# A two-layer encoder kernel: one more pair of feed-forward tiles in seven products, and earlier query weights

## The reference, cut to what matters

```python
def swiglu(h, w_gu, w_down):
    u = h @ w_gu
    return (jax.nn.silu(u[..., :D_FF]) * u[..., D_FF:]) @ w_down

def swa_sink_attention(hn, w_q, sinks, w_o, k, v):
    ...
    s = jnp.einsum('bcqkgd,bcwkd->bckgqw', q, kw).astype(jnp.float32) * (HEAD_DIM ** -0.5)
    ...
    m = jnp.maximum(jnp.max(s, axis=-1, keepdims=True), sink)
    p = jnp.exp(s - m)
    p = p / (jnp.sum(p, axis=-1, keepdims=True) + jnp.exp(sink - m))
    o = jnp.einsum('bckgqw,bcwkd->bcqkgd', p.astype(vw.dtype), vw)
    return o.reshape(B, S, N_Q_HEADS * HEAD_DIM) @ w_o
```

## Time and profile before

| | us |
|---|---|
| median of 3 runs | 1071.61 |
| lowest and highest run | 1071.55, 1072.2 |
| the profiled execution's own time | 1071.88 |
| its span, first to last instruction | 1070.1 |
| TensorE busy | 1059.6 |
| VectorE busy | 858.9 |
| ScalarE busy | 618.9 |
| GpSimd busy | 52.3 |

### The profile page before, as it was taken

The page is one execution under the profiler, slowest core; times in us unless marked ns, Lnnn a source line. Parts: engine busy times, 40 slices in busy tenths (PEclk is TensorE's granted clock), DMA queues, the critical chain, the costliest instruction groups (busy, mean ns, idle before and its releaser), DMA issues.

```text
span 1070.1 us, 17761 instructions
## 1 busy us (share of the span) xinstructions
PE 1059.6 (99%) x6817; PEld 953.7 (89%) x6817; DVE 858.9 (80%) x1310; ACT 618.9 (58%) x1127; POOL 52.3 (5%) x86
## 2 busy tenths in 40 slices
PE   8999999999999999999999999999999999999997
PEld 7887887889999999998888988889999999998886
DVE  5878987688888888889877589568888888889874
ACT  6376574555466666656556587555455555556553
POOL 1000000000112222100010100000000000000000
PEclk9999999999999999999999999999999999999999
DMA  6332233242346556462234201152234334352211
GB/s 210 99 109 70 79 110 119 79 118 73 119 135 188 155 171 194 132 228 89 79 99 153 65 2 40 45 152 64 90 105 119 96 103 119 92 201 102 79 40 79
DMA packets 137142, 117.74 MB, mean 110 GB/s; under 512 B 8305, under 2 KB 123105, under 8 KB 137058
## 3 DMA queue, kind: packets, MB, share of 16 engines
q1 hardware_dynamic: 133600, 106.12, 32.1%
q0 software_dynamic: 3456, 10.49, 2.9%
q10 hardware_dynamic: 2, 0.00, 0.0%
HBM read 109.25 MB, written 7.34 MB: 109 GB/s over the span
## 4 chain that ended last, share of the span: by engine, by line
PE 97%; DVE 1%; ACT 1%; issue 0%; DMA 0%; DVEq 0%; ACTq 0%
PE ps L2389 12%; PE ps L2387 12%; PE ps L2385 12%; PE ps L2047 8%; PE ps L2048 8%; PE ps L2049 8%; PE ps L2067 7%; PE ps L2073 7%; PE ps L2069 7%; PE ps L2103 4%; PE ps L2101 4%; PE ps L2102 4%; PE ps L2316 1%; PE ps L2080 1%; PE ps L2491 1%; PE ps L2519 1%
## 5 line engine op out<-in xcount | busy, mean ns | idle before, releaser
L2385 PE MATMUL ps<-t_hi,w_hi 128*128 128x256 f32 x608 | 172.1, 283 | 0.0
L2387 PE MATMUL ps<-t_lo,w_hi 128*128 128x256 f32 x608 | 172.1, 283 | 0.0
L2389 PE MATMUL ps<-t_hi,w_lo 128*128 128x256 f32 x608 | 172.1, 283 | 0.0
L2047 PE MATMUL ps<-x_hi,w_hi 128*128 128x512 f32 (+1 forms) x384 | 137.1, 357 | 0.3 <-DVE w_lo L1382 0.2
L2048 PE MATMUL ps<-x_lo,w_hi 128*128 128x512 f32 (+1 forms) x384 | 135.1, 352 | 0.0
L2049 PE MATMUL ps<-x_hi,w_lo 128*128 128x512 f32 (+1 forms) x384 | 135.0, 352 | 0.0
L1382 DVE TENSOR_TENSOR w_lo<-raw,w_hi 128x1024 fp32r<-128x1024 f32 x73 | 89.0, 1223 | 54.2 <-ACT w_hi L836 53.9
L2389 PE MATMUL ps<-x_hi,w_lo 128*128 128x256 f32 x456 | 129.0, 283 | 0.0
L2387 PE MATMUL ps<-x_lo,w_hi 128*128 128x256 f32 x456 | 129.0, 283 | 0.0
L2385 PE MATMUL ps<-x_hi,w_hi 128*128 128x256 f32 x456 | 129.0, 283 | 0.0
L2385 PEld LDWEIGHTS ps<-t_hi,w_hi 128*128 128x128 f32 x608 | 116.7, 192 | 0.0
(11 more groups left out here) (288 smaller groups left out, 2587.5 us busy)
## 6 DMA issues: line engine op xcount, KB each, us to landing
raw<-in_ffn_w_gu SPq DMA_DIRECT2D x88, 512.0 KB, 4.8
raw<-in_ffn_w_down SPq DMA_DIRECT2D x28, 512.0 KB, 4.2
raw<-in_a_w_in SPq DMA_DIRECT2D x24, 512.0 KB, 3.9
raw<-in_a_w_out SPq DMA_DIRECT2D x12, 512.0 KB, 3.9
scaled_kv_q<-part POOLq DMA_DIRECT2D x20, 256.0 KB, 3.8
part<-in_b_w_q POOLq DMA_DIRECT2D x32, 128.0 KB, 2.8
xr<-in_ffn_w_down SPq DMA_DIRECT2D x8, 512.0 KB, 7.7
raw<-in_b_w_o SPq DMA_DIRECT2D x16, 256.0 KB, 4.0
```

What stands on the lines that cost most here:

```text
L2047: nc.tensor.matmul(out_ps, hi_w, hi_x, start=first, stop=False)
L2385: nc.tensor.matmul(ps[:, b, 0:HS], w_hi[:, slot, cols], hi, start=start, stop=False, skip_group_check=True)
L2387: nc.tensor.matmul(ps[:, b, 0:HS], w_hi[:, slot, cols], lo, start=False, stop=False, skip_group_check=True)
L2389: ins = nc.tensor.matmul(ps[:, b, 0:HS], w_lo[:, slot, cols], hi, start=False, stop=j == DC // 2 - 1, skip_group_check=True)
```

## The change

1. PLAIN is 2 instead of 3: in each layer the third plain pair becomes the first in seven products, so there are 20 of these. The banks follow: `seven_banks(c)` gives 0, 1, 2, then 3, 4, 5, then 6, 7, 2 for the first three pairs, and the pairs behind alternate as before. The sums of x_f's first half and two weight sums are now made in the boundary (`whole_x`, `weight_sum_3`, `weight_sum_2`), ahead of the last x_low.
2. The low halves of tiles T+2 and T+3 of each layer are no longer subtracted on VectorE. ScalarE writes the rounded negative of the tile into `w_lo`, and a DMA from GpSimd's queue adds `raw` to it. TensorE and SyncE wait for that DMA (w_lo_landed). ScalarE's split of T+3 goes ahead of x_high(b, 2).
3. The query tiles T_Q+2 and T_Q+3 are split around the keys; T_Q+4's cast goes ahead of the table load of the exponential; queries 1 are split on VectorE altogether (`q_both(1, 2)`), row_max(1) goes ahead of the first division, and T_Q+5's cast behind the exponentials.
4. The table of Silu is loaded by a small activation at the start of the feed-forward, and three semaphores of constants are made one.

```diff
-PLAIN = 3
+PLAIN = 2
...
+def low_by_dma(t):
+
+    return any(t - T_GU[f] in (2, 3) for f in range(2))
...
+def seven_banks(c):
+
+    if c == 2:
+        return 6, 7, 2
+    first = 3 * ((c + (c > 2)) % 2)
+    return first, first + 1, first + 2
...
+            def add_raw(t):
+
+                pool.wait_ge(w_neg_ready, dma_lows(t))
+                nc.gpsimd.dma_start(w_lo[:, t % 4, :], raw[:, t % 4, :], accum_op=ALU.add)\
+                    .then_inc(w_lo_landed[t % 4], 16)
+
+            add_raw(T_GU[0] + 2)
+            add_raw(T_GU[0] + 3)
             pool.wait_ge(hid_ready, 2)
...
                     nc.scalar.copy(halves(t)[0], raw_of(t)).then_inc(w_hi_ready, 1)
+                if low_by_dma(t):
+                    nc.scalar.mul(halves(t)[1], raw_of(t), -1.0).then_inc(w_neg_ready, 1)
...
                 post(b, 3)
+                if b != 1:
+                    split_hi(n + 4)
                 x_high(b, 2)
                 pre(b, 3)
-                split_hi(n + 4)
+                if b == 1:
+                    split_hi(n + 4)
                 x_high(b, 3)
...
+            split_hi(T_Q + 2)
             act.wait_ge(tiles_done, upto(T_KV))
             act.wait_ge(kpad_ready, 1)
             nc.scalar.mul(k_hi[:, CHUNK:], bank(0), HD ** -0.5).then_inc(khi_ready, 1)
-            split_hi(T_Q + 2)
+            split_hi(T_Q + 3)
...
             q_high(0)
-            split_hi(T_Q + 3)
+            split_hi(T_Q + 4)
             nc.scalar.activation(std[:, 35:36], eps[:, 0:1], ACT.Exp)
...
             ins.then_inc(vdiag_ready, 1)
-            split_hi(T_Q + 4)
-            q_high(1)
...
                 split_lo(n + 4)
+                if b != 1:
+                    whole_x(b // 2, 0)
+                    weight_sum_3(b // 2, 0)
+                    weight_sum_2(b // 2, 0)
                 x_low(b, 3)
...
+            split_lo(T_Q + 2)
             dve.wait_ge(khi_ready, 1)
...
+            split_lo(T_Q + 3)
+
             def q_both(m, parts):
...
             q_low(0)
-            split_lo(T_Q + 2)
...
                 if half == 0:
-                    q_low(1)
+                    q_both(1, 2)
             biased(1, 0)
             biased(1, 1)
+            row_max(1)
...
             def tile_ready(t):
-                pe.wait_ge(w_lo_ready, upto(t))
+                if low_by_dma(t):
+                    pe.wait_ge(w_hi_ready, upto(t))
+                    pe.wait_ge(w_lo_landed[t % 4], 16 * dma_lows_in_place(t))
+                else:
+                    pe.wait_ge(w_lo_ready, lows_upto(t))
```

More of the change, by code:

```diff
@@ L162, in fixed, with lows_upto, dma_lows, dma_lows_in_place @@
     return len(FIXES) * f + FIXES.index(name) + 1
+def low_by_dma(t):
+    return any(t - T_GU[f] in (2, 3) for f in range(2))
+def lows_upto(t):
+    return sum(pair_of_seven(i) is None and chunk_place(i) is None and not low_by_dma(i) for i in range(t + 1))
+def dma_lows(t):
+    return sum(low_by_dma(i) for i in range(t + 1))
+def dma_lows_in_place(t):
+    return sum(low_by_dma(i) for i in range(t % 4, t + 1, 4))
+def seven_banks(c):
[3 more added lines that the diff above has]
+    return first, first + 1, first + 2
 def plain_row(f, k):
@@ L493, in trunk @@
         w_lo_ready = sem("w_lo_ready")
+        w_neg_ready = sem("w_neg_ready")
+        w_lo_landed = {place: sem(f"w_lo_landed{place}") for place in (2, 3)}
         tiles_done = sem("tiles_done")
@@ L1323, in _ @@
                     o_high(m // 2 - 1, 0)
-                if m >= 0 and T_Q + m + 5 < T_O + 4:
+                if m > 0 and T_Q + m + 5 < T_O + 4:
                     split_hi(T_Q + m + 5)
@@ L1336, in _ @@
                     p_high(m, 1)
+                if m == 0:
+                    split_hi(T_Q + 5)
             o_high(PAIRS_H // 2 - 1, 1)
@@ L1582, in after_pre, with whole_x, weight_sum_3, weight_sum_2 @@
                                        op1=ALU.mult).then_inc(hn_ready, 1)
+            def whole_x(f, half):
+                dve.wait_ge(xlo_ready, 2 * TC * f + 2 * half + 2)
+                tok = slice(HS * half, HS * half + HS)
+                for ks in (slice(0, 4), slice(4, 8)):
+                    v.tensor_tensor(x_f[:, ks, tok], x_hi[:, ks, tok].bitcast(F32), x_lo[:, ks, tok].bitcast(F32),
+                                    ALU.add).then_inc(xf_ready, 1)
+            def weight_sum_3(f, c):
+                gate_t = T_GU[f] + 2 * (PLAIN + c)
+                n = SEVEN * f + c
+                for t in (gate_t, gate_t + 1):
+                    dve.wait_ge(raw_landed[t % 4], raw_count(t))
+                if n > 0:
+                    dve.wait_ge(lo_s, n)
+                v.tensor_tensor(work[:, 0, 0:HW], raw[:, gate_t % 4, 0:HW], raw[:, (gate_t + 1) % 4, 0:HW], ALU.subtract)\
+                    .then_inc(s3_ready, 1)
+            def weight_sum_2(f, c):
+                n = SEVEN * f + c
+                dve.wait_ge(s3_ready, n + 1)
+                if n > 0:
+                    dve.wait_ge(s4_ready, n)
+                v.tensor_tensor(work[:, 0, HW:], raw[:, (T_GU[f] + 2 * (PLAIN + c) + 1) % 4, HW:], work[:, 0, 0:HW],
+                                ALU.subtract).then_inc(s2_ready, 1)
             def boundary(b):
@@ L1614, in gated @@
                     v.tensor_tensor(hid[:, n, :], hid[:, n, :], bank(2 * n % 8 + 1), ALU.mult).then_inc(hid_ready, 1)
-                def whole_x(half):
-                    dve.wait_ge(xlo_ready, 2 * TC * f + 2 * half + 2)
-                    tok = slice(HS * half, HS * half + HS)
-                    for ks in (slice(0, 4), slice(4, 8)):
-                        v.tensor_tensor(x_f[:, ks, tok], x_hi[:, ks, tok].bitcast(F32), x_lo[:, ks, tok].bitcast(F32),
-                                        ALU.add).then_inc(xf_ready, 1)
                 low, high = slice(0, DC // 2), slice(DC // 2, DC)
@@ L1849, in ffn @@
                         weight_sums(c + 1)
+                    if c == 0:
+                        a_low(c + 1)
                     gate_1(c)
-                    if not last:
+                    if c == 0:
+                        pass
+                    elif not last:
                         a_low(c + 1)
@@ L1993, in _ @@
                     o_low(m // 2 - 1, 1)
[L1994 to L1996 removed]
+                if 0 < m < PAIRS_H - 1:
                     biased(m + 1, 0)
@@ L2008, in _ @@
                     q_both(m + 2, 2)
-                    split_lo(T_Q + 3 + 3 * m // 2)
+                    if m > 0:
+                        split_lo(T_Q + 3 + 3 * m // 2)
                     divided(m + 1)
```

106 lines of the change are left out of this document (50 added, 56 removed).

## The result

The changed kernel takes 1076.68 us (median of 5 runs, 1076.09 to 1077.18), the kernel before 1071.76 (5 runs beside them, 1071.55 to 1072.2): a ratio of 1.0046, 95% interval 1.0031 to 1.006, so 4.9 us slower. The profiled execution took 1077.18 us, its span is 1075.3.

The account below looks back on a forecast made before the run. TensorE, busy 99% of the span, was taken as the bound. +3.8 us in attention less 0.55 in the layers gave +3.2 on 1071.61: 1074.8 us; own range 1073.0 to 1076.5, with 1072.6 to 1079.0 holding about 0.8.

Parts of the forecast that it names:

- both waits: At the keys, TensorE waits 1.3 us for q_lo ahead of scores(0) and about 2.4 us for v_diag.
- The low end of the forecast's own range: Whole kernel: 1073.0 us, with 2.9 us lost in attention and nothing given back in the layers.
- The plain pair: Each layer: seven products replace a plain pair, saving 0.83 us; VectorE's late gate tile at pair 1 gives back 0.55.
- The wait of 0.25 at the second half of the tokens: Each layer: x_lo ends at 256.8, TensorE wants it at 256.63 and waits about 0.25 us, inside the 0.55.
- The adding DMAs: Low halves of T+2 and T+3: 5.6 us per 512 KB, T+2 0.5 late, costing nothing beyond the 0.55.
- Rival (a): Adding DMAs in the layers land late: 1078.5 us if they take 7.5, 1082.9 if 9.7; chance 0.20.
- scores(0), 1.3 late: At the keys: T_Q+3's split goes ahead of the first queries, so TensorE waits 1.3 us for q_lo(0).
- v_diag, 2.45 more: At the values: T_Q+4's cast and the table load precede v_diag, so TensorE waits 2.45 us more, 3.75 late altogether.
- Gaps of the old size behind it: Attention behind v_diag: TensorE's gaps, 0.9 us together before, remain of the old size, so the loss stays 3.8.
- a sign of being wrong: TensorE's granted clock falling below 1.00 in the new waits; listed as disproof, given no size in the sum.

Follow-up runs that it names:

- load_held: layers_alone with SyncE's load of T+6 held until T+3's low half has landed; 1071.88 us, one execution.
- combined: Changed kernel with both orders at the keys undone, T+2/T+3 negatives before casts, pair 1's low half before its weight sums, T+6's load waiting for the cast too; 1071.62 us.
- sums_on_gpsimd: combined with the first two weight sums of pair 0 moved from VectorE to GpSimd; 1071.43 us.
- layers_alone: Kernel before plus only the two layers' change (two plain pairs, two low halves by adding DMA), attention as before; 1071.73 us.
- keys_alone: Kernel before plus only the attention-stage change, with three plain pairs and no adding DMA; 1076.17 us.
- queries_first: Changed kernel with both halves of the first queries ahead of T_Q+3's split on ScalarE and VectorE; 1075.29 us.
- filled_wait: queries_first plus 18 products of 256 columns, changing no output, keeping TensorE busy in the wait for v_diag; 1073.73 us.
- both_filled: Changed kernel plus 12 products ahead of scores(0) and 18 ahead of the turned values, changing no output; 1076.32 us.
- table_first: queries_first with the exponential's table load and small exponential ahead of T_Q+4's split; 1072.71 us.
- both_first: Changed kernel with first queries ahead of T_Q+3's split and v_diag ahead of T_Q+4's split; 1071.44 us.

## Why the prediction was right, and where its sum was short

The forecast was 1074.8 with a range of 1072.6 to 1079.0, and slower with 0.83. The direction, the place and both waits were right; the time came out 1.9 us longer. (The low end of the forecast's own range is 1071.61 + 2.9 - 1.66 = 1072.85 and not 1073.0, which changes nothing.) By its steps:

- **The plain pair, -0.83 per layer, 0.55 given back.** Measured: 0.17 and 0.26 kept in after, where 0.28 was forecast. That the row of VectorE sets it is shown: taking away one wait or both ahead of it (load_held, combined) left the layer at 350.7, taking work out of the row (sums_on_gpsimd) shortened it. The row's length was near: its end at pair 1's gate tile was forecast for 277.2 and is 278.28 on a timeline that by then is 0.98 later. Of the 0.66 given back in layers_alone 0.4 is at T+3 and the rest in pairs 0 and 1. -0.55 was forecast for both layers, -0.43 measured. The wait of 0.25 at the second half of the tokens didn't show, though x_lo ended when the sum had it (256.8, measured 257.74 on the later timeline): T+3's addition had held TensorE just ahead of it. In combined, without that, it showed.
- **The adding DMAs, 5.6 us taken, T+2 0.5 late.** Half right. T+3 takes 5.4 to 5.6, but T+2 4.4 or 4.5, in time by 0.3 us. The Trainium skill's fit (DMA: Bandwidth & Descriptors, "Anatomy of one DMA — SWDGE (gpsimd) path") gave an estimated 4.4 us with the bytes counted twice, and the trace agrees with it for an addition that runs alone; for the one behind it, it is 1.0 short. That their delay costs nothing more, since VectorE is late anyway, was right. Rival (a) held in one boundary of 22.
- **scores(0), 1.3 late.** 1.42 by the stages, in all four kernels that keep this order.
- **v_diag, 2.45 more.** 2.50 by the stages, in keys_alone, queries_first, filled_wait and both_filled alike; its split into cast and load was tested in table_first.
- **Gaps of the old size behind it.** Right: 18.43 against 18.36. The gap at 621.87 went, as forecast, and those at the transposes of p are 0.55 and 0.53, since VectorE reaches the divisions no sooner.
- **No term for the clock.** This is what the sum lacked: it took every product of the stage at 2.4 GHz, though its last paragraph named a fall as a sign of being wrong, and that sign came. It cost 0.6 us in the profiled execution of the changed kernel, 1.0 in keys_alone, and 1.3 in queries_first.

The stages give 4.2 us for the change: 3.25 forecast, +0.6 for the clock, +0.3 for the three terms of waits and gaps together, +0.1 in the layers. The medians say 4.9. The 0.7 between is not settled. In the profiled execution the first weight tile was there late and TensorE lost 1 us in the first 13:

```profile
9.74 1.05 ACT L877 CAST w_hi<-raw 128x1024 fp32r<-128x1024 f32 x1 [2.22 <-DMA raw<-in_a_w_in]
```

But its cast starts anywhere from 7.16 to 9.74 in the profiled executions of the fourteen kernels, whose first loads are the same, so one execution says nothing of the medians. The medians of the parts add up within their intervals: 4.5 for keys_alone and 0.0 for layers_alone, against 4.9.

**No version is told from before.** both_first, combined and sums_on_gpsimd have medians 0.2 to 0.4 us below that of before in their groups, all inside 0.2%. By stages the last is 1.09 us shorter in the layers and 0.12 longer behind the keys.
